# Strassen's algorithm for gate tiles of three float32 feed-forwards on one Trainium2 core

## The chip, the cores and the metric
One core of one Trainium2 chip runs the whole program. The metric is the device time of one execution in microseconds, as the median of the runs; less is better.

## What is computed
A sequence of 512 tokens of width 1024, in float32, goes through two blocks: a first one (pooling mixer, spatial gating, a feed-forward with a short convolution, a gated projection) and a second one of two layers, each with a SwiGLU feed-forward, attention, and another SwiGLU feed-forward. The change is about the last three of these four SwiGLU feed-forwards, called s1, s2 and s3 in the kernel (s0 is the first):

```python
D_FF = 2816
def swiglu(h, wg, wu, wd):
    return (jax.nn.silu(h @ wg) * (h @ wu)) @ wd
...
x = x + 0.5 * swiglu(rmsnorm_2(x, ffn_norm2[i]), ffn2_wg[i], ffn2_wu[i], ffn2_wd[i])
```

## The kernel before, in words
**Data.** The activations stay in SBUF transposed: `X` is 8 chunks of 128 channels by 512 tokens. A float32 product is made of three fp32r products: every operand is split into a high part (a ScalarE copy that rounds, `Hh`, `Ph`, `Wh`) and a low part (the rest, by a VectorE subtraction, `Hl`, `Pl`, `Wl`), and `mm3` (L1186 to L1188) issues high x low, low x high and high x high. `H` holds the normed input of a feed-forward, `P` the hidden activations.

**Weights.** All weights are a list of tiles of 1 MB at most (`weight_tiles`). SyncE loads tile n into `RAW[n % 2]` as soon as the low part of tile n - 2 is made (L2632). The step `split` makes its high part on ScalarE in two halves (L1565) and its low part on VectorE (L1928; on GpSimd, L2495, in the attention stages) into region n % 3 of `Wh` and `Wl`, once tile n - 3 is used up.

**A feed-forward** (`ffn`, L338) goes through the 22 chunks of 128 hidden channels in `THIRDS` of 8, 8 and 6. A third is first four (or three) pairs: pair (h, j) takes a gate tile `a` and a value tile `b`, each 1024 x 256, and makes two banks of each, a bank being 128 hidden channels by 512 tokens, from 8 k-blocks x 3 = 24 matmuls (`dense`). Then come four down-projection tiles `d`, whose two banks each are added to `X` (`add_x`, L2160).
For every pair: VectorE multiplies each bank by the norm factor R (`scale`, L1995; R lies in `M[:, 6]` and is made at the start of the feed-forward, ScalarE's part of it is L1611); ScalarE applies silu from the bank into a `TMP` tile (`silu`, L1682); VectorE multiplies by the value bank (`glu`, L2139); ScalarE makes the high half in `Ph` (`pair`, L1628), VectorE the low half in `Pl` (L1916).

**What sets the order.** `order` writes one list of steps by hand; each engine's program goes through the same list and issues its own part of every step. So each engine works strictly in the order of the list, and a step that waits keeps everything behind it on its engine waiting. Semaphore waits are worked out from named events. PSUM banks (8) and `TMP` tiles (3) are taken from rings; a taker waits until the last holder is done. Small other work is put in between: `norm_step` after each bank (in the last third of s3 it is `x_turn`, four PE transposes at L1362 and a ScalarE copy at L1706), and `extra` before a pair (in s1 the steps `trig` and `tables`, L2191 to L2227, before pair (0, 1)).
The sums of squares for the next norm are added on GpSimd (`stats`, L2502; a second sum L2509). Other lines in the rows: L1821 and L2450 are a ScalarE copy and a VectorE subtraction of half a bank in the second attention, L2169 and L2174 VectorE operations of the stage before s0.

## Time and profile before
| | us |
|---|---|
| median of 3 runs | 2660.2 |
| lowest, highest run | 2658.64, 2660.27 |
| profiled execution, first to last instruction (span) | 2659.0 |
| PE busy in the span | 2630.2 |
| DVE, ACT, POOL busy | 1437.9, 987.7, 320.2 |

The profiler's own execution is given by its span; the page lists no other time of it, and the runs' times stand beside it. PE is TensorE (PEld its weight loads), DVE VectorE, ACT ScalarE, POOL GpSimd, SP SyncE. Matmuls are pipelined: a row's duration is longer than the step from one start to the next, and it is the step (the pitch) that adds up to the span. The page gives times by engine, by line and by group of instructions; the timelines give single instructions with their start; "idle before <- releaser" names what an engine waited for.

### The profile page before, as it was taken

The numbers are of one execution on the slowest core, as the hardware profiler recorded it, in microseconds if no ns is written. First come the engines' busy times: TensorE is split into PE (matmuls) and PEld (weight loads), VectorE is DVE, ScalarE is ACT, GpSimd is POOL, SyncE is SP. The second block draws the span as 40 slices with busy tenths as digits, with TensorE's granted clock in tenths as the row PEclk, the third lists the DMA queues.
The fourth block names the chain that finished last, engine by engine and source line by source line (L and its number), as shares of the span: only waits on it lengthen the run. The fifth ranks groups of instructions, "written<-read, shape, count | busy, mean of one in ns | idle before, by whom it ended". The sixth has DMA issues, their size and how long they took to land.

```text
span 2659.0 us, 30833 instructions
## 1 busy us (share of the span) xinstructions
PE 2630.2 (99%) x12546; PEld 2197.8 (83%) x12560; DVE 1437.9 (54%) x2266; ACT 987.7 (37%) x1626; POOL 320.2 (12%) x388
## 2 busy tenths in 40 slices
PE   9999999999999999999999999999999989999999
PEld 8888888888887788889988888888888788888887
DVE  7637547574757444356774343453434676543433
ACT  4334334242454222246642222422223586432221
POOL 0000010000021000015530000100000586200000
PEclk9999999999999999999999999999999999999999
DMA  5332225423232444453323222232222101232222
GB/s 161 121 101 80 95 79 190 154 85 106 80 101 90 107 103 107 98 109 104 104 96 110 95 95 88 88 111 95 95 95 83 61 19 42 88 109 95 95 91 68
DMA packets 276389, 258.91 MB, mean 97 GB/s; under 512 B 40324, under 2 KB 266647, under 8 KB 276247
## 3 DMA queue, kind: packets, MB, share of 16 engines
q1 hardware_dynamic: 276231, 256.93, 31.6%
q8 instruction: 99, 1.62, 0.2%
q14 instruction: 43, 0.35, 0.0%
q10 hardware_dynamic: 16, 0.00, 0.0%
HBM read 242.23 MB, written 14.68 MB: 97 GB/s over the span
## 4 chain that ended last, share of the span: by engine, by line
PE 90%; DVE 3%; ACT 3%; issue 2%; POOL 2%; DMA 0%; SPq 0%; POOLq 0%; DVEq 0%; ACTq 0%
PE bank L1186 29%; PE bank L1188 29%; PE bank L1187 29%; PE bank L1353 1%; DVE Wl L1928 1%; ACT Wh L1565 0%; PE bank L1417 0%; POOL Wl L2495 0%; ACT Z L1851 0%; POOL TMP L2502 0%; DVE Pl L2450 0%; PE bank L1285 0%; PE bank L1513 0%; ACT Hh L1841 0%; PE bank L1197 0%
## 5 line engine op out<-in xcount | busy, mean ns | idle before, releaser
L1186 PE MATMUL bank<-Hh,Wl 128*128 128x512 f32 x2136 | 838.9, 393 | 0.8 <-DVE Hl L1947 0.8
L1188 PE MATMUL bank<-Hh,Wh 128*128 128x512 f32 x2136 | 832.3, 390 | 0.0
L1187 PE MATMUL bank<-Hl,Wh 128*128 128x512 f32 x2136 | 831.8, 389 | 0.0
L1928 DVE TENSOR_TENSOR Wl<-RAW,Wh 128x1024 fp32r<-128x1024 f32 (+2 forms) x420 | 493.7, 1219 | 171.2 <-ACT Wh L1565 170.4
L1565 ACT ACTIVATE Wh<-RAW 128x1024 fp32r<-128x1024 f32 (+2 forms) x454 | 441.2, 1022 | 382.8 <-PE bank L1188 358.4
L1186 PEld LDWEIGHTS bank<-Hh,Wl 128*128 128x128 f32 x2136 | 401.4, 188 | 86.8 <-issue 1.7
L1187 PEld LDWEIGHTS bank<-Hl,Wh 128*128 128x128 f32 x2136 | 401.5, 188 | 84.0 <-issue 1.7
L1188 PEld LDWEIGHTS bank<-Hh,Wh 128*128 128x128 f32 x2136 | 401.2, 188 | 83.9
L1186 PE MATMUL bank<-Ph,Wl 128*128 128x512 f32 x1152 | 451.9, 392 | 0.8 <-DVE Wl L1928 0.5
L1188 PE MATMUL bank<-Ph,Wh 128*128 128x512 f32 x1152 | 448.6, 389 | 0.0
L1187 PE MATMUL bank<-Pl,Wh 128*128 128x512 f32 x1152 | 448.2, 389 | 0.0
L1995 DVE TENSOR_TENSOR bank<-bank,M 128x512 f32<-128x512 f32 x220 | 150.6, 697 | 387.9 <-PE bank L1188 379.2
L2502 POOL TENSOR_TENSOR TMP<-TMP 128x512 f32<-128x512 f32 x56 | 78.2, 1396 | 1822.1 <-ACT TMP L1592 1820.9
L1186 PEld LDWEIGHTS bank<-Ph,Wl 128*128 128x128 f32 x1152 | 216.3, 188 | 47.4 <-DVE Wl L1928 0.9
L1188 PEld LDWEIGHTS bank<-Ph,Wh 128*128 128x128 f32 x1152 | 216.2, 188 | 45.4
L2160 DVE SCALAR_TENSOR_TENSOR X<-bank,X 128x512 f32<-128x512 f32 x168 | 114.9, 688 | 256.3 <-PE bank L1188 255.7
L1187 PEld LDWEIGHTS bank<-Pl,Wh 128*128 128x128 f32 x1152 | 216.3, 188 | 44.7 <-issue 0.2
L1628 ACT ACTIVATE Ph<-TMP 128x512 fp32r<-128x512 f32 x110 | 69.5, 632 | 463.6 <-DVE TMP L2139 410.4
L1682 ACT ACTIVATE TMP<-bank 128x512 f32<-128x512 f32 x88 | 52.2, 599 | 224.4 <-DVE bank L1995 224.3
L1916 DVE TENSOR_TENSOR Pl<-TMP,Ph 128x512 fp32r<-128x512 f32 x126 | 87.2, 692 | 77.6 <-ACT Ph L1628 76.8
L1583 ACT ACTIVATE Hh<-X,P 128x512 fp32r<-128x512 f32 x64 | 45.7, 722 | 102.5 <-DVE X L2160 101.1
L2495 POOL TENSOR_TENSOR Wl<-RAW,Wh 128x1024 fp32r<-128x1024 f32 (+1 forms) x34 | 74.6, 2216 | 27.4 <-ACT Wh L1565 23.2
(336 smaller groups left out, 2427.4 us busy)
## 6 DMA issues: line engine op xcount, KB each, us to landing
RAW<-in_ffn_wg SPq DMA_DIRECT2D x44, 1024.0 KB, 5.2
RAW<-in_ffn_wu SPq DMA_DIRECT2D x44, 1024.0 KB, 5.2
RAW<-in_ffn_wd SPq DMA_DIRECT2D x32, 1024.0 KB, 4.8
RAW<-in_w_up SPq DMA_DIRECT2D x22, 1024.0 KB, 5.1
RAW<-in_w_in SPq DMA_DIRECT2D x20, 1024.0 KB, 5.1
RAW<-in_ffn_wd SPq DMA_DIRECT2D x16, 768.0 KB, 4.3
bias_scratch<-M SPq DMA_DIRECT2D x16, 512.0 KB, 8.0
RAW<-in_w_down SPq DMA_DIRECT2D x8, 1024.0 KB, 4.8
```

The lines of the kernel that those rows point to most:

```text
L1186: mm(o, ll, rh, start=start, stop=False)
L1187: mm(o, lh, rl, start=False, stop=False)
L1188: return mm(o, lh, rh, start=False, stop=stop)
L1565: run(Wh[:, n % 3, x:y], RAW[:, n % 2, x:y], ACT.Copy).then_inc(*w_hi.up(("w_hi", n, i)))
L1628: run(Ph[:, q, :], tmp(name) if src == "tmp" else bank(name), ACT.Copy).then_inc(*pair_hi.up(("p_hi", q, ver)))
L1682: run(vacant(t), bank(b), ACT.Silu).then_inc(*act_out.up(("silu", t), free=b))
L1916: tt(Pl[:, q, :], src, f(Ph[:, q, :]), ALU.subtract).then_inc(*pair_lo.up(("p", q, ver), free=free))
L1928: tt(Wl[:, n % 3, x:y], RAW[:, n % 2, x:y], f(Wh[:, n % 3, x:y]), ALU.subtract).then_inc(*w_lo.up(*([("w_lo", n)] if i else [])))
L1995: tt(bank(b), bank(b), RVIEW[norm_R[nv]], ALU.mult).then_inc(*dve_out.up(("scaled", b)))
L2160: stt(X[:, c, :], bank(b), factor, X[:, c, :], ALU.mult, ALU.add).then_inc(*x_new.up(("x", ver, c), free=b))
L2495: tt(Wl[:, n % 3, x:y], RAW[:, n % 2, x:y], f(Wh[:, n % 3, x:y]), ALU.subtract).then_inc(*w_lo_pool.up(*([("w_lo", n)] if i else [])))
L2502: tt(SQ, SQ, tmp(("t_sq", nv, c)), ALU.add).then_inc(*pool_out.up(("sq", nv, c), free=("t_sq", nv, c)))
```

## The change
In s1, s2 and s3 the gate tiles from pair (0, 2) on are computed by one level of Strassen's algorithm (Winograd's form). The tile's k-blocks, its 256 hidden channels and the 512 tokens are each halved, and instead of eight block products there are seven (`PRODUCTS`), each of 4 k-blocks x 3 matmuls of 256 columns. They need four sums of weight blocks (`w_sum`, `w_sum4`, on GpSimd, from `RAW`), four sums of activation blocks for each r (`hc_sum`, made once at the start of a feed-forward, on GpSimd for even r and on VectorE for odd r, from scaled float32 copies `hc_raw` that ScalarE makes, and split into high and low by `hc`), and sums of the results. The results are built up in three half-used banks: fx takes products 1, 6, 7 and 4 one on top of the other, with ScalarE copying it away in between (`cp`), fz takes product 2, fy 5 and 3; VectorE adds the pieces (`c11`, `c12`, `c22`) into `TMP`, GpSimd multiplies by R there (`rm`; `c21` has it with it), and silu runs in place (`silu_f`). PE's products 6, 7 and 4 wait for the copies 1, 2 and 3, and product 3 for c22.

The value tiles and the down projection keep their matmuls. The order of the steps is new (`ffn_seven` for `ffn`). The weight regions are handed out differently (`places`): in a feed-forward value tiles always have the region `other`, gate tiles the region `mid`, and the fourth piece of a Strassen tile goes into `WS`. `Ph` and `Pl` 8 to 15 hold the activation sums, so a third always uses `P` 0 to 7. `feed` issues the sums and splits of gate tile n + 2 during pair n. The diff, cut:

```diff
+SEVEN = ("s1", "s2", "s3")
+FIRST_SEVEN = (0, 2)
+PRODUCTS = {1: (0, 0, 0, "fx"), 2: (0, 1, 1, "fz"), 3: (3, 0, 2, "fy"), 4: (2, 1, 6, "fx"), 5: (1, 0, 3, "fy"),
+            6: (1, 1, 5, "fx"), 7: (2, 0, 4, "fx")}
+PIECE_DONE = {0: (1, 2), 1: (5, 6), 2: (7, 4), 3: (3,)}
```

The regions (`places`) and the new helpers of `order`:

```diff
+        tag, x = name[:-1], name[-1]
+        if tag not in SEVEN:
+            regions = regions[1:] + regions[:1]
+            pieces = [(2048 * regions[2], 2048)]
+        else:
+            if x == "a" and key == (0, 0):
+                mid, other, ends = regions
+            if is_seven(tiles[n]):
+                pieces = [(2048 * ends + 1024 * side, 1024), (2048 * mid, 1024), (2048 * mid + 1024, 1024)]
+                side = 1 - side
+            else:
+                region = mid if x == "a" else other if x == "b" else (ends, mid, other, ends)[key[1]]
+                pieces = [(2048 * region, 2048)]
+            if x == "d" and key[1] == 3:
+                if key[0] < 2:
+                    other, ends = ends, other
+                else:
+                    regions = [mid, other, ends]
...
+
+    def feed(n, *pieces):
+        for piece in pieces if n < NW and is_seven(tiles[n]) else ():
+            if piece == "sums":
+                do("w_sum", n)
+                continue
+            if piece == 3:
+                do("w_sum4", n)
+            do("w_fill", n, piece)
+            if piece == 3:
+                assert now["split"] == n
+                now["split"] += 1
+                load()
+
+    def plain(n):
+        if n < NW and not is_seven(tiles[n]) and now["split"] == n:
+            split()
+            load()
 
     def norm_step():
```

The new order of a feed-forward (`...` stands for lines left out):

```diff
+    def ffn_seven(tag, nver=None, after=None, after_base=0):
+        do("mark", ("up", tag))
+        gname, gbase = GAINS[tag]
+        keys = hkeys()
+        combos = []
+        for r in range(4):
+            combos.append(lambda r=r: do("hc_raw", tag, r, xv[2 * r:2 * r + 2], gname, gbase))
+            combos.append(lambda r=r: do("hc_sum", tag, r))
+        for z, r in ((4, 0), (7, 1), (10, 2), (11, 3)):
+            combos.insert(z, lambda r=r: do("hc", tag, r))
+
...
+        def prod(n, i):
+            if i in (1, 2, 5):
+                banks.take((PRODUCTS[i][3], n))
+            do("prod", n, i, tag, keys)
+
+        def pair_seven(h, j, last_pair):
+            n = next_tile(tag + "a", (h, j), 0)
+            t = [("t_a", tag, h, j, c) for c in range(2)]
+            feed(n + 2, "sums")
+            prod(n, 1)
+            prod(n, 2)
+            for c in range(2):
+                tmps.take(t[c])
+            do("cp", n, 1, t)
+            plain(n + 1)
+            do("c11", n, t)
+            norm_step()
+            prod(n, 6)
+            do("cp", n, 2, t)
+            prod(n, 5)
+            prod(n, 7)
+            do("cp", n, 3, t)
+            do("c22", n, t)
+            norm_step()
+            nb = next_tile(tag + "b", (h, j), 0)
+            bb = [(tag + "b", h, j, c) for c in range(2)]
+            if last_pair:
+                plain(n + 2)
+            else:
+                feed(n + 2, 0, 1)
+            dense([bb[0]], nb, 8, "H")
+            scale([bb[0]])
+            prod(n, 4)
+            do("c21", n, t, now["norm"])
+            prod(n, 3)
+            do("c12", n, t)
+            for m in range(2):
+                do("rm", n, m, t, now["norm"])
+            dense([bb[1]], nb, 8, "H", kw=1)
+            do("used", nb)
+            if last_pair:
+                plain(n + 3)
+            else:
+                feed(n + 2, 2, 3)
+            for m in range(2):
+                do("silu_f", n, m, t)
+            for m in range(2):
+                if m:
+                    scale([bb[1]])
+                do("glu", t[m], bb[m])
+                pair_p(2 * j + m, "tmp", t[m], ("glu", t[m]))
+
+        def pair_eight(h, j):
+            begins = (h, j) == (0, 0)
+            ba, bb = ([(tag + x, h, j, c) for c in range(2)] for x in "ab")
+            na = next_tile(tag + "a", (h, j), 1)
+            dense(ba, na, 8, "H", scaled=not begins, wide=begins)
+            do("used", na)
+            if begins:
+                norm_step()
+                combine(2)
+                nb = next_tile(tag + "b", (h, j), 1)
+                feed(na + 2, "sums")
+                dense(bb[0:1], nb, 8, "H")
+                combine(2)
+                dense(bb[1:2], nb, 8, "H", kw=1)
+                do("used", nb)
+                scale(ba)
+                feed(na + 2, 0)
+            for c in range(2):
+                t = tmps.take(("t_a", tag, h, j, c))
+                do("silu", ba[c], t)
+            if begins:
+                combine(2)
+                feed(na + 2, 1, 2, 3)
+                scale(bb)
+            else:
+                nb = next_tile(tag + "b", (h, j), 1)
+                feed(na + 2, "sums", 0)
+                combine(3)
+                dense(bb[0:1], nb, 8, "H")
+                scale(bb[0:1])
+                feed(na + 2, 1)
+                combine(2)
+                dense(bb[1:2], nb, 8, "H", kw=1)
+                do("used", nb)
+                feed(na + 2, 2, 3)
+                scale(bb[1:2])
+            for c in range(2):
+                t = ("t_a", tag, h, j, c)
+                do("glu", t, bb[c])
+                pair_p(2 * j + c, "tmp", t, ("glu", t))
+            if begins:
+                combine(2)
+
+        for h, (c0, n) in enumerate(THIRDS):
+            last = (tag, h) == ("s3", 2)
+            if last:
+                todo[:] = [lambda i=i: x_turn(i // 4, i % 4) for i in range(8)]
+            for j in range(n // 2):
+                if (h, j) != (0, 0):
+                    extra(4)
+                if (h, j) >= FIRST_SEVEN:
+                    assert not combos
+                    pair_seven(h, j, j == n // 2 - 1)
+                else:
+                    pair_eight(h, j)
+            if h == 2:
+                h_new(tag + "_after")
+                do("mark", ("mfree", tag))
+            for i in range(4):
+                extra(4)
+                nd = next_tile(tag + "d", (h, i))
+                if last:
+                    out_rows(i, nd, n // 2, 0)
+                    continue
+                bd = [(tag + "d", h, i, c) for c in range(2)]
+                dense(bd, nd, n, "P", base=0, wide=i == 0)
+                do("used", nd)
+                if h < 2 and i == 2:
+                    feed(nd + 2, "sums", 1, 2)
+                if h < 2 and i == 3:
```

What the engines do for the new steps, PE first, then ACT, DVE and POOL:

```diff
+            elif kind == "prod":
+                n, i, tag, keys = s
+                piece, part, x, region = PRODUCTS[i]
+                name = (region, n)
+                begins = i in (1, 2, 5)
+                pe.wait_ge(*at(("w_lo", n, piece)))
+                o = (vacant(name) if begins else bank(name))[:, 0:256]
+                if i == 6 or i == 7 or i == 4:
+                    pe.wait_ge(*at(("cp", n, {6: 1, 7: 2, 4: 3}[i])))
+                elif i == 3:
+                    pe.wait_ge(*at(("c22", n)))
+                wh, wl = (w[:, 512 * part:512 * part + 512] for w in piece_of(n, piece))
+                for r in range(4):
+                    pe.wait_ge(*at(("hc_lo", tag, r) if x > 2 else keys[2 * r + min(x, 1)]))
+                    xh, xl = moving(r, x)
+                    rr = slice(128 * r, 128 * r + 128)
+                    mm(o, wl[:, rr], xh, start=begins and r == 0, stop=False, skip_group_check=True)
+                    mm(o, wh[:, rr], xl, start=False, stop=False, skip_group_check=True)
+                    ins = mm(o, wh[:, rr], xh, start=False, stop=r == 3, skip_group_check=True)
+                ins.then_inc(*bank_full.up(("prod", n, i)))
...
+            elif kind == "w_fill":
+                n, piece = s
+                act.wait_ge(*at(("sum", n, piece) if piece else ("raw", n)))
+                for event in released(n, piece):
+                    act.wait_ge(*at(event))
+                if piece == 3:
+                    all_gone(("up", tiles[n][0][:-1]))
+                run(shaped(piece_of(n, piece)[0], piece), piece_source(n, piece), ACT.Copy).then_inc(
+                    *w_hi.up(("w_hi", n, piece)))
+            elif kind == "hc_raw":
+                tag, r, xver, gname, base = s
+                for c in (2 * r, 2 * r + 1):
+                    act.wait_ge(*at(("x", xver[c % 2], c)))
+                all_gone(("up", tag))
+                if r > 1:
+                    act.wait_ge(*at(("hc_lo", tag, r - 2)))
...
+            elif kind == "hc":
+                tag, r = s
+                act.wait_ge(*at(("hc_raw", tag, 2 * r + 1)))
+                act.wait_ge(*at(("hc_sum", tag, r)))
+                all_gone(("up", tag))
+                run(Ph[:, 8 + 2 * r:10 + 2 * r, :], hc_sums(r), ACT.Copy).then_inc(*pair_hi.up(("hc_hi", tag, r)))
+            elif kind == "cp":
+                n, k, t = s
+                m = int(k == 3)
+                act.wait_ge(*at(("prod", n, {1: 1, 2: 6, 3: 7}[k])))
+                v = tmp(t[m]) if k == 2 else vacant(t[m])
+                z = 0 if k == 1 else 256
+                run(v[:, z:z + 256], bank(("fx", n))[:, 0:256], ACT.Copy).then_inc(*act_out.up(("cp", n, k)))
+            elif kind == "silu_f":
+                n, m, t = s
+                act.wait_ge(*at(("rm", n, m)))
+                act.wait_ge(*at(("c21", n)))
+                run(tmp(t[m]), tmp(t[m]), ACT.Silu).then_inc(*act_out.up(("silu", t[m])))
...
+            elif kind == "w_fill":
+                n, piece = s
+                wh, wl = piece_of(n, piece)
+                dve.wait_ge(*at(("w_hi", n, piece)))
+                tt(shaped(wl, piece), piece_source(n, piece), f(shaped(wh, piece)), ALU.subtract).then_inc(
+                    *w_lo.up(("w_lo", n, piece), *([("w_lo", n)] if piece == 3 else [])))
...
+            elif kind == "hc":
+                tag, r = s
+                q = slice(8 + 2 * r, 10 + 2 * r)
+                dve.wait_ge(*at(("hc_hi", tag, r)))
+                tt(Pl[:, q, :], hc_sums(r), f(Ph[:, q, :]), ALU.subtract).then_inc(*pair_lo.up(("hc_lo", tag, r)))
...
+            elif kind == "c22":
+                n, t = s
+                v = tmp(t[1])[:, 256:512]
+                dve.wait_ge(*at(("cp", n, 3)))
+                dve.wait_ge(*at(("prod", n, 5)))
+                tt(v, bank(("fy", n))[:, 0:256], v, ALU.add).then_inc(*dve_out.up(("c22", n)))
+            elif kind == "c12":
+                n, t = s
+                v = tmp(t[0])[:, 256:512]
+                dve.wait_ge(*at(("cp", n, 2)))
+                dve.wait_ge(*at(("prod", n, 3)))
+                tt(v, bank(("fy", n))[:, 0:256], v, ALU.add).then_inc(*dve_out.up(("c12", n), free=("fy", n)))
...
+            elif kind == "w_sum":
+                n, = s
+                v = raw_blocks(n)
+                a11, a21, a22 = v[:, :, 0, 0, :], v[:, :, 0, 1, :], v[:, :, 1, 1, :]
+                n1, n2 = (NS[:, z:z + 512].rearrange("p (r m) -> p r m", r=4) for z in (0, 512))
+                pool.wait_ge(*at(("raw", n)))
+                for event in gone(("up", tiles[n][0][:-1])):
+                    pool.wait_ge(*event)
+                if seven_before(n) is not None:
+                    pool.wait_ge(*at(("w_lo", seven_before(n), 1)))
+                tt(n1, a21, a22, ALU.add).then_inc(*w_sum.up(("sum", n, 0)))
+                pool.wait_ge(*at(("sum", n, 0)))
+                tt(n2, n1, a11, ALU.subtract).then_inc(*w_sum.up(("sum", n, 1)))
+                tt(a21, a11, a21, ALU.subtract).then_inc(*w_sum.up(("sum", n, 2)))
+            elif kind == "w_sum4":
+                n, = s
+                a12 = raw_blocks(n)[:, :, 1, 0, :]
+                n2 = NS[:, 512:1024].rearrange("p (r m) -> p r m", r=4)
+                pool.wait_ge(*at(("sum", n, 1)))
+                pool.wait_ge(*at(("w_lo", n, 0)))
+                tt(a12, a12, n2, ALU.subtract).then_inc(*w_sum.up(("sum", n, 3)))
...
+            elif kind == "rm":
+                n, m, t, nv = s
+                z = 256 * m
+                v = tmp(t[m])[:, z:512]
+                pool.wait_ge(*at(("c22", n) if m else ("c12", n)))
+                if m == 0:
+                    pool.wait_ge(*at(("c11", n)))
+                pool.wait_ge(*at(("R", nv)))
+                tt(v, v, RVIEW[norm_R[nv]][:, z:512], ALU.mult).then_inc(*pool_out.up(("rm", n, m)))
```

The sums over the activation blocks:

```diff
+    def combos(eng, tt, out_, tag, r):
+
+        b11_12, b21_22 = ((tag, 2 * r), (tag, 2 * r + 1))
+        eng.wait_ge(*at(("hc_raw",) + b11_12))
+        tt(hc_block(r, 4), hc_block(r, 1), hc_block(r, 0), ALU.subtract).then_inc(*out_.up(("hc_t1", tag, r)))
+        eng.wait_ge(*at(("hc_raw",) + b21_22))
+        tt(hc_block(r, 5), hc_block(r, 3), hc_block(r, 1), ALU.subtract).then_inc(*out_.up())
+        eng.wait_ge(*at(("hc_t1", tag, r)))
+        tt(hc_block(r, 6), hc_block(r, 3), hc_block(r, 4), ALU.subtract).then_inc(*out_.up(("hc_t2", tag, r)))
+        eng.wait_ge(*at(("hc_t2", tag, r)))
+        tt(hc_block(r, 7), hc_block(r, 2), hc_block(r, 6), ALU.subtract).then_inc(*out_.up(("hc_sum", tag, r)))
```

## Rows read from the trace of the kernel before
**Rows 1.** the page: busy time of the engines, and the chain that ended last
```profile
PE 2630.2 (99%) x12546; PEld 2197.8 (83%) x12560; DVE 1437.9 (54%) x2266; ACT 987.7 (37%) x1626; POOL 320.2 (12%) x388
...
PE 90%; DVE 3%; ACT 3%; issue 2%; POOL 2%; DMA 0%; SPq 0%; POOLq 0%; DVEq 0%; ACTq 0%
```
**Rows 2.** table by stretches, s1: busy us (x instructions), granted clock, DMA share, GB/s
```profile
1364.90:1725.80 360.90, 360.90 (x1598) 298.57 (x1596) 165.93 (x227) 103.24 (x132) 9.41 (x7) 1.00 0.30 98
```
**Rows 3.** timeline of PE in s1: start us, us, engine, line, operation
```profile
1499.65 0.39 PE L1188 MATMUL bank<-Hh,Wh 128*128 128x512 f32 x1
...
1511.89 0.39 PE L1188 MATMUL bank<-Hh,Wh 128*128 128x512 f32 x1
```
**Rows 4.** timeline of PE in the first attention, half-width matmuls
```profile
1227.21 0.28 PE L1186 MATMUL bank<-Wh,Hl 128*128 128x256 f32 x1
...
1229.97 0.28 PE L1188 MATMUL bank<-Wh,Hh 128*128 128x256 f32 x1
```
**Rows 5.** groups by line and form in s1, busy us, mean ns, idle before
```profile
L1565 ACT ACTIVATE Wh<-RAW 128x1024 fp32r<-128x1024 f32 x60 | 60.0, 1049 | 69.7 <-PE bank L1188 63.4 <-DMA RAW<-in_ffn_wu 6.3
...
L1928 DVE TENSOR_TENSOR Wl<-RAW,Wh 128x1024 fp32r<-128x1024 f32 x60 | 71.3, 1232 | 22.0 <-ACT Wh L1565 22.0
```
**Rows 6.** groups by line and form, whole span, operations of 256 columns
```profile
L1821 ACT ACTIVATE TMP<-bank 128x256 f32<-128x256 f32 x16 | 6.2, 385 | 1.1 <-DVE pkf L2392 1.0
...
L2450 DVE TENSOR_TENSOR Pl<-bank,Ph 128x256 fp32r<-128x256 f32 x16 | 6.6, 415 | 0.7 <-ACT Ph L1860 0.7
```
**Rows 7.** groups by line and form, POOL: in s1, and over the span
```profile
L2502 POOL TENSOR_TENSOR TMP<-TMP 128x512 f32<-128x512 f32 x7 | 9.4, 1344 | 348.9 <-ACT TMP L1592 348.9
...
L2495 POOL TENSOR_TENSOR Wl<-RAW,Wh 128x1024 fp32r<-128x1024 f32 x26 | 62.2, 2417 | 22.4 <-ACT Wh L1565 18.2 <-DVE M L2276 2.8 <-DVE sm L2317 1.4
```
**Rows 8.** timeline of DVE and POOL where both read two SBUF tensors
```profile
787.01 0.80 DVE L2169 TENSOR_TENSOR TMP<-TMP,M 128x512 f32<-128x512 f32 x1 [1.79 <-ACT TMP L1701]
...
787.22 1.75 POOL L2509 TENSOR_TENSOR Z<-Z,TMP 128x512 f32<-128x512 f32 x1
...
787.84 1.67 DVE L2174 TENSOR_TENSOR X<-X,TMP 128x512 f32<-128x512 f32 x1
```
**Rows 9.** timeline of DVE and ACT, the end of a pair in s1
```profile
1508.24 0.70 DVE L1995 TENSOR_TENSOR bank<-bank,M 128x512 f32<-128x512 f32 x1 [4.74 <-PE bank L1188]
...
1508.85 0.68 DVE L2139 TENSOR_TENSOR TMP<-TMP,bank 128x512 f32<-128x512 f32 x1
...
1509.56 0.63 ACT L1628 ACTIVATE Ph<-TMP 128x512 fp32r<-128x512 f32 x1 [8.97 <-DVE TMP L2139]
...
1510.22 0.69 DVE L1916 TENSOR_TENSOR Pl<-TMP,Ph 128x512 fp32r<-128x512 f32 x1 [0.70 <-ACT Ph L1628]
```
**Rows 10.** timelines of DVE and ACT, first two pairs of s1, s2, s3
```profile
1382.27 0.16 DVE L2191 CAST sm<-smi 128x4 f32<-128x4 int32 x1
...
1387.01 2.36 DVE L1928 TENSOR_TENSOR Wl<-RAW,Wh 128x1024 fp32r<-128x1024 f32 x2
...
1733.09 0.60 ACT L1611 ACTIVATE M<-bank 128x512 f32<-128x512 f32 x1 [5.18 <-PE bank L1301]
...
1738.57 0.70 DVE L1995 TENSOR_TENSOR bank<-bank,M 128x512 f32<-128x512 f32 x1 [2.34 <-PE bank L1188]
...
2314.97 0.60 ACT L1611 ACTIVATE M<-bank 128x512 f32<-128x512 f32 x1 [9.61 <-PE bank L1301]
...
2325.90 0.70 DVE L1995 TENSOR_TENSOR bank<-bank,M 128x512 f32<-128x512 f32 x1 [0.61 <-PE bank L1188]
```
**Rows 11.** timeline, one x_turn in the last third of s3: PE, then ACT
```profile
2577.40 0.60 PE L1362 MATMUL bank<-ident,X 128*128 128x128 f32 x4
...
2578.04 0.60 ACT L1706 ACTIVATE M<-bank 128x512 f32<-128x512 f32 x1 [5.33 <-PE bank L1362]
```
**Rows 12.** table by stretches, after the ple stage and in the second attention
```profile
823.00:827.00 4.00, 4.00 (x17) 3.36 (x17) 3.69 (x13) 0.14 (x1) 0.00 (x0) 0.66 0.75 236
2115.00:2135.00 20.00, 14.65 (x115) 13.79 (x114) 15.40 (x45) 17.80 (x54) 17.23 (x28) 1.00 0.16 54
```

135 lines of the change are left out of this document (115 added, 20 removed).

## The prediction
> **What bounds the kernel now.** The page first: TensorE (PE) is busy 99% of the span of 2659.0 us, and the chain that ended last runs through it for 90% [rows 1]. Then the table by stretches: over s1, the first of the three feed-forwards that the change touches, PE is busy for all of 360.90 us at granted clock 1.00, VectorE (DVE) for 165.93, ScalarE (ACT) for 103.24 and GpSimd (POOL) for 9.41 [rows 2]. The waits list no wait of PE from 1364 to 2082 us nor from 2302 us on. So in these stages the time is the number of matmuls times their pitch, and everything else has slack. A busy PE isn't the whole story of the change, though: it makes PE wait for ACT in the middle of a pair, so the order of ACT's and DVE's queues has to be read as well.
>
> **What is saved.** Pitch is start to start. With 512 columns: 54 steps from 1499.65 to 1511.89 us, 0.2267 us each [rows 3]. With 256 columns: 23 steps from 1227.21 to 1229.97, 0.120 us each [rows 4]; the half-size matmul costs 53%, not 50%. A gate tile was 48 matmuls of 512 columns, 10.88 us; it becomes 7 products of 12 matmuls of 256 columns, 84 x 0.120 = 10.08 us. Saved: 0.80 us. Nine of the 11 pairs of each feed-forward are treated so, three times: 27 x 0.80 = 21.6 us. That is all the change can bring, 0.8%.
>
> The Trainium skill, "TensorE: Matmul & The Clock Gate", section "Back-to-back issue gap", gives N/2.4 + 2.5 ns for a warm matmul. By it the tile would save 1.19 us and the change 32 us, called an estimate; both traced pitches are above that rule, so the traced ones are taken.
>
> **What a pair does to the queues.** Set t = 0 at the first product of a pair. PE: products 1 and 2 (1.44 us each) to 2.88; 6, 5, 7 to 7.20; first value bank to 12.64; products 4, 3 to 15.52; second value bank to 20.96. Product 6 adds to the bank that ACT must first have copied (cp 1). That copy stands in ACT's queue behind the whole tail of the pair before, so I follow that tail from the end of product 3 (pitch end X) to cp 1 of the next pair. PE leaves 8.32 us for it (second value bank 5.44, products 1 and 2 2.88). Durations stand in [rows 5 to 7, 9]; a follower on the same engine starts 0.09 before the former's end, one on another engine 0.03 to 0.05 after it:
> - c12 on DVE starts at X+0.19 (last matmul's tail and hop), as scale does after its bank; 0.42.
> - w_fill 2's low half is next on DVE (its inputs are ready) and starts at X+0.52, before POOL's rm 0, which waits for c12's end. It takes 1.22 and reads two SBUF tensors, as rm 0 does. [Rows 8] shows what that means: DVE's TMP,M operation at 787.01 stretches POOL's of 787.22 to 1.75 instead of 1.34 us [rows 7], so that this one really begins 0.18 before DVE's recorded end; and the next DVE one, at 787.84, waits for POOL (1.67 instead of 0.69). One instruction at a time has the path. So rm 0 really starts at X + 0.52 + 1.22 - 0.18 = X+1.56.
> - rm 0 1.34, rm 1 (256 columns, 0.81 by the slope between 512 and 1024), w_sum4 1.34, less two overlaps, and the hop to ACT: X+5.02.
> - ACT w_fill 3 high 0.63, DVE its low half 0.69 (ACT's silu runs beside it): X+6.37. Then glu 0, pair high 0, pair low 0, scale and glu 1, pair high 1: 0.59+0.66+0.72+0.52+0.68+0.66; together X+10.20.
> - cp 1 0.39 less 0.09, hop 0.05: X+10.55.
>
> PE therefore waits 10.55 - 8.32 = 2.2 us at product 6. Nothing behind it makes this good, for the same chain starts again at product 3: a pair takes 20.96 + 2.2 = 23.2 us, where it took 96 x 0.2267 = 21.76. Inside the pair I find no further wait over 0.2 us: cp 2 has product 5 to hide under, cp 3 and c22 the first value bank, and the value tile's split ends just before its bank is due.
>
> The skill's "SBUF — State Buffer", section "Who interferes with whom", says that a DVE instruction with two SBUF inputs contends with a GpSimd one that reads SBUF, the later one waiting for the whole of the other. That rule speaks against this change, and [rows 8] bear it out. Without the effect rm 0 would start at X+0.69, 0.87 us sooner, and the sum below would be 14 us less.
>
> **How often.** Such a tail precedes a Strassen pair 6 times in a feed-forward: once in third 0, three times in third 1, twice in third 2. After down projections ACT's queue is empty and cp 1 is in time. The last pair of a third hides its tail under the first six of eight (or four of six) k-blocks of the down projection, 8.2 or 5.4 us. Of the 18, two are worse: in s3's last third an x_turn follows each dense call, so ACT waits for the four transposes behind the second value bank (0.60) and copies (0.60) [rows 11] before it may start w_fill 2, 3 and silu. Worked through in the same way these two cost 4.5 and 4.9 us. Sum: 16 x 2.2 + 9.4 = 44.6 us.
>
> **The first two pairs.** They now carry the activation sums: 8 ACT copies like a pair's high half (0.63 [rows 9]), four of 1.05 [rows 5], 8 combinations of 0.42 [rows 6] and four low halves of 1.23 [rows 5] on DVE, 8 combinations of 0.8 [rows 7] on POOL. And the value tile of pair (0,1) now shares a region with that of (0,0), so its split comes only after all this. In s2, the last value bank of pair (0,0) ends at 1738.57 - 0.19; the tile is due 10.88 us later, at 1749.26. From the copy of R, which stood at 1733.09 [rows 10], the queue has two copies, four combinations, two scales, hc 0, raw 2, two glu/pair rounds, hc 1 and the two Wl halves: done at 1749.2. Just in time, but POOL's three weight sums (4.0 us) now fall into the same 5 us, and with one reader at a time two of them delay it: 2.6 us late. In s1 the trig steps stand before the split (1382.27 to 1387.01 [rows 10]): 4.7 late. In s3 R comes later (2314.97) and the tile is due at 2325.71 [rows 10]: 3.4, with the sums 6.0. Together 13.3 us.
> After that DVE has 10.9 us of work under 10.9 us of matmuls, then scale, glu 0, pair, glu 1, pair, cp 1, 4.2 + 1.3 us against the 2.88 of products 1 and 2: 2.6 us at each of three feed-forwards, 7.8.
>
> **The sum.** 44.6 + 13.3 + 7.8 - 21.6 = +44.1 us: the profiled span 2659.0 becomes 2703. The median, 2660.2, stands 1.2 us above the profiled span, so I forecast 2704 us.
>
> Bounds. POOL's operations are untraced for these operands: with the one-tensor-and-column form they could be shorter, and if the collision with w_fill 2 and with the sums fell away the forecast drops by 14 + 5 us, to 2685. If also the beginnings hid themselves, 2666. Upwards: POOL operations of 1.64, between the 1.34 and the 1.75 of [rows 7, 8], add 0.3 x 3 x 16 = 14 us. A halved clock is the other one: after PE's weak stretch at 822 us the granted clock is 0.66 in the mean of 4 us, so at its lower level, 1.2 GHz, for most of them, with some 1.4 us lost; against it, 14.65 busy in 20 us with waits up to 2.3 left it at 1.00 [rows 12]. None is in the sum; one for each of some seven long waits adds 10 us. An unseen gain in the beginnings has no room, PE not having waited there.
>
> **Rivals.**
> A. The tail hides: POOL and ACT are early enough, or the order leaves cp 1 free, and only 21.6 us of matmuls are left out: 2660.2 - 21.6 = 2639, faster. For it: DVE is 46% and ACT 29% busy in s1 [rows 2], so there is ample capacity. Against it: the wait is one of order, not of capacity. The point from which it decides: all waits together must be under 21.6 us, that is under 0.8 us a pair; my chain has 2.2 and would need to be 1.4 us shorter everywhere and the beginnings nearly free.
> B. Near break-even: no collision on the read path and no waits at the beginnings, chain 1.2 us late: 16 x 1.2 + 9.4 for the x_turns + 3 x 1.0 - 21.6 = +10, 2670; with a little less, no measurable change.
> C. Clock drops at every wait of 2.2 us too: 16 x 1.4 + 10 more, about 2736. For it: row 823 to 827; against it: the attention stretch.
> D. The 256-column matmuls are held by weight loads, one for each, at a pitch above 0.120. At 0.130 the saving is gone (84 x 0.130 = 10.92) and the time about 2727. [Rows 4] speak against it: these matmuls too change their weights every time.
>
> **How the numbers follow.** Forecast with its bounds (2685 to 2730) 0.64; rival A 0.12; B 0.13, of which 0.05 within 0.2%; C 0.05; D 0.06. 0.2% (5.3 us) is about what a measurement of this kernel can tell from no change. Faster 0.12, same 0.05, slower 0.83. The range for 8 in 10 leaves out A and C and reaches into B: 2665 to 2734.
>
> **What would show it.** Right: PE waits for ACT (the copy of bank fx) some 16 times at 2 to 2.5 us and longer twice in s3's last third; ahead of each such copy ACT's pair copy, ahead of that DVE's glu; POOL's rm 0 listed at 2.2 us rather than 1.3 where it starts behind w_fill 2; PE waits for DVE Wl once in each feed-forward's second pair; matmuls of 256 columns at 0.12; each feed-forward about 15 us longer. Wrong: no PE wait at product 6, feed-forwards of 353 us instead of 360; waits that sit at product 7 or 4 or at the value bank would mean that another link is late; a granted clock under 0.98 in the stages would be C.

## The result: 2734.0 us, and the profile after

The changed kernel takes 2734.0 us in the median of five runs (2733.0 to 2736.7), against 2660.2 for the kernel before: a ratio of 1.028, 95% interval 1.0267 to 1.0292. The direction was as forecast; the forecast was +44 us, the outcome +74. The profiled execution is the longest of the five (2736.7 us) and has a span of 2735.5 us, 76.5 more than before's 2659.0.

The page of the changed kernel, busy times and the chain that ended last, beside [rows 1]:

```profile
PE 2645.6 (97%) x13532; PEld 2254.5 (82%) x13532; DVE 1572.2 (57%) x2410; ACT 1084.5 (40%) x1797; POOL 598.2 (22%) x574
...
PE 70%; issue 9%; DVE 7%; POOL 7%; ACT 4%; DMA 3%; POOLq 0%; SPq 0%; ACTq 0%; DVEq 0%
```

TensorE is busy 15 us longer, though 21.6 us of its work were to be saved. That is the first sign that something besides waiting has been added. The second is the granted clock in the table by stretches of s1 and s3 (columns as in [rows 2]: busy of PE, PEld, DVE, ACT, POOL, then the clock), where [rows 2] had 1.00:

```profile
1364.90:1736.00 371.10, 349.22 (x1860) 303.34 (x1859) 206.07 (x270) 131.56 (x183) 98.14 (x66) 0.98 0.30 94
...
2350.00:2735.50 385.50, 356.92 (x1879) 310.27 (x1877) 191.73 (x224) 120.76 (x169) 87.81 (x58) 0.96 0.26 85
```

The waits of PE (engine line <- releaser: us in all, times, longest). L1564 is the first matmul of a product, L1464 that of a dense bank:

```profile
PE bank L1564 <- ACT TMP L1897: 43.9, 18, 5.0
PE bank L1464 <- DVE Wl L2267: 17.3, 7, 7.1
...
PE bank L1564 <- issue: 4.4, 3, 1.5
```

L1897 is the copy cp 1. It is waited for 18 times: 16 times for 2.15 us, and in s3's last third for 4.53 and 4.97 us. The other nine waits in s1 to s3 belong to the first pairs: 7.10, 1.47 and 0.42 us in s1, 2.36, 1.48 and 0.84 in s2, 5.84, 1.48 and 0.34 in s3 (the smallest of each at the first value bank of pair (0,2)). All 27 make 16 x 2.15 + 9.50 + 21.33 = 65.2 us.

Here is one tail, link by link, merged from the timelines of the four engines in s1:

```profile
1517.82 0.42 DVE L2301 TENSOR_TENSOR TMP<-bank,TMP 128x256 f32<-128x256 f32 x1 [1.01 <-PE bank L1566]
1518.16 1.22 DVE L2273 TENSOR_TENSOR Wl<-RAW,Wh 128x1024 fp32r<-128x1024 f32 x1
1518.32 2.91 POOL L2908 TENSOR_TENSOR TMP<-TMP,M 128x512 f32<-128x512 f32 x2 [12.36 <-DVE TMP L2301]
1521.19 1.29 POOL L2895 TENSOR_TENSOR RAW<-RAW,M 128x512 f32<-128x512 f32 x1
1522.51 0.63 ACT L1872 ACTIVATE WS<-RAW 128x512 fp32r<-128x512 f32 x1 [5.01 <-POOL RAW L2895]
1523.18 0.69 DVE L2273 TENSOR_TENSOR WS<-RAW,WS 128x512 fp32r<-128x512 f32 x1 [3.80 <-ACT WS L1872]
1523.79 0.68 DVE L2518 TENSOR_TENSOR TMP<-TMP,bank 128x512 f32<-128x512 f32 x1
1524.50 0.63 ACT L1965 ACTIVATE Ph<-TMP 128x512 fp32r<-128x512 f32 x1 [0.31 <-DVE TMP L2518]
...
1527.22 0.63 ACT L1965 ACTIVATE Ph<-TMP 128x512 fp32r<-128x512 f32 x1 [2.09 <-DVE TMP L2518]
1527.76 0.37 ACT L1897 ACTIVATE TMP<-bank 128x256 f32<-128x256 f32 x1
...
1528.27 0.36 PE L1564 MATMUL bank<-Ph,Wl 128*128 128x256 f32 x1 [2.15 <-ACT TMP L1897]
```

c12, w_fill 2's low half, rm 0 and rm 1 (one row, x2), w_sum4, w_fill 3, glu 0, pair high 0, pair high 1, cp 1, product 6: the order of the prediction, nothing in another place. ACT stands idle for 5.01 us and again for 2.09 us in it, and DVE for 3.80: waits of order, while all three engines have room.

What the prediction had not in its sum is seen behind such a wait. PE's timeline behind the wait that ends at 1438.87, and behind the one of 1528.27:

```profile
1438.87 0.35 PE L1564 MATMUL bank<-Ph,Wl 128*128 128x256 f32 x1 [2.15 <-ACT TMP L1897]
...
1440.01 0.41 PE L1564 MATMUL bank<-Ph,Wl 128*128 128x256 f32 x1
1440.23 0.41 PE L1565 MATMUL bank<-Pl,Wh 128*128 128x256 f32 x1
...
1528.94 0.28 PE L1566 MATMUL bank<-Ph,Wh 128*128 128x256 f32 x1
1529.06 0.28 PE L1564 MATMUL bank<-Ph,Wl 128*128 128x256 f32 x1
```

The step from start to start is 0.12 us in the second case and 0.213 in the first: the lower clock level, 1.2 GHz, for 15 matmuls (1439.37 to 1442.57), and 1.57 us lost with the slower first ones. In the table by stretches the same two places read 0.66 and 1.00 (the column behind POOL's):

```profile
1438.00:1443.00 5.00, 4.13 (x22) 4.16 (x23) 3.39 (x4) 3.01 (x5) 0.00 (x0) 0.66 0.16 49
1528.00:1533.00 5.00, 4.73 (x38) 4.72 (x39) 4.37 (x4) 2.51 (x5) 3.66 (x2) 1.00 0.08 26
```

The two waits are equally long. Of the 16 of 2.15 us, 8 are followed by the lower clock; so are all five longer ones (2.36 to 7.10 us), with 1.7 to 3 us lost behind each. And each wait costs 0.15 us more than the row lists as idle: the last start before 1528.27 is 2.43 us earlier, 2.31 more than the pitch.

**The balance.** The matmuls should take 21.6 us less, the waits add 65.2 and the restarts 27 x 0.15 = 4.1. Of the 76.5 us that leaves 76.5 + 21.6 - 65.2 - 4.1 = 28.8 us. The slow matmuls of the timelines give 8 x 1.57 = 12.6, and 2.2, 1.7, 3.0, 3 and 2.75 behind the five long waits, together about 25. The rest, some 3.5 us, lies in part outside s1 to s3: the copy of R in s1, which stands at 1372.20 us in the profile before, stands at 1373.81 here, behind a stretch of lower clock that before's profile hasn't (0.76 over 1243 to 1250 us, where before has 1.00) in a stage that the change doesn't touch. In the other kernels' profiles that copy stands between 1370.8 and 1372.5, so I take this for a difference between executions.

```profile
1243.00:1250.00 7.00, 5.43 (x33) 5.44 (x34) 4.95 (x17) 4.58 (x16) 4.00 (x6) 0.76 0.93 255
```

What is left are matmuls slower by 0.1 us right behind a wait and what I can't assign. From the copy of R in s1 to that in s2 it is 23.8 us more than before, from there to that in s3 (with the second attention) 18.0, and from there to the end 33.1; the forecast had about 15 for each feed-forward.

### The profile page after: what moved, and what is told of

The parts are those of the page before. It is cut to its first block, busy times and chain, and to the rows that moved or that the text cites. A ratio compares the mean times of both kernels' runs of the same rounds, so it can differ in the third digit from the quotient of the medians.

```text
span 2735.5 us, 33395 instructions
## 1 busy us (share of the span) xinstructions
PE 2645.6 (97%) x13532; PEld 2254.5 (82%) x13532; DVE 1572.2 (57%) x2410; ACT 1084.5 (40%) x1797; POOL 598.2 (22%) x574
## 4 chain that ended last, share of the span: by engine, by line
PE 70%; issue 9%; DVE 7%; POOL 7%; ACT 4%; DMA 3%; POOLq 0%; SPq 0%; ACTq 0%; DVEq 0%
PE bank L1464 21%; PE bank L1466 21%; PE bank L1465 21%; DMA RAW<-in_ffn_wg 3%; PE bank L1564 1%; PE bank L1565 1%; PE bank L1566 1%; POOL M L2887 1%; POOL TMP L2908 1%; POOL M L2885 1%; POOL RAW L2895 1%; DVE Wl L2267 1%; POOL RAW L2888 1%; PE bank L1651 1%; DVE bank L2374 1%
## 5 line engine op out<-in xcount | busy, mean ns | idle before, releaser
L1464 PE MATMUL bank<-Hh,Wl 128*128 128x512 f32 x1704 | 674.7, 396 | 17.7 <-DVE Wl L2267 16.9
L1465 PE MATMUL bank<-Hl,Wh 128*128 128x512 f32 x1704 | 667.0, 391 | 0.0
L1466 PE MATMUL bank<-Hh,Wh 128*128 128x512 f32 x1704 | 666.5, 391 | 0.0
L2267 DVE TENSOR_TENSOR Wl<-RAW,Wh 128x1024 fp32r<-128x1024 f32 (+1 forms) x366 | 473.1, 1335 | 138.2 <-ACT Wh L1864 137.6
L1464 PE MATMUL bank<-Ph,Wl 128*128 128x512 f32 x1152 | 451.9, 392 | 0.8 <-DVE Wl L2267 0.4
L1464 PEld LDWEIGHTS bank<-Hh,Wl 128*128 128x128 f32 x1704 | 322.2, 189 | 87.8 <-DVE Wl L2267 19.2
L1466 PEld LDWEIGHTS bank<-Hh,Wh 128*128 128x128 f32 x1704 | 321.7, 189 | 68.5
L1465 PEld LDWEIGHTS bank<-Hl,Wh 128*128 128x128 f32 x1704 | 322.3, 189 | 65.7 <-issue 1.7
L1464 PEld LDWEIGHTS bank<-Ph,Wl 128*128 128x128 f32 x1152 | 216.3, 188 | 47.1 <-DVE Wl L2267 0.9
L1564 PE MATMUL bank<-Ph,Wl 128*128 128x256 f32 x432 | 131.9, 305 | 48.3 <-ACT TMP L1897 43.9
L2908 POOL TENSOR_TENSOR TMP<-TMP,M 128x512 f32<-128x512 f32 (+1 forms) x54 | 83.8, 1572 | 355.1 <-DVE TMP L2301 355.1
L1564 PEld LDWEIGHTS bank<-Ph,Wl 128*128 128x128 f32 x432 | 90.9, 210 | 53.0 <-issue 52.0
```

The lines of the kernel that those rows point to most:

```text
L1464: mm(o, ll, rh, start=start, stop=False)
L1465: mm(o, lh, rl, start=False, stop=False)
L1466: return mm(o, lh, rh, start=False, stop=stop)
L1564: mm(o, wl[:, rr], xh, start=begins and r == 0, stop=False, skip_group_check=True)
L2267: tt(wflat(Wl, o + x, o + y), RAW[:, n % 2, x:y], f(wflat(Wh, o + x, o + y)), ALU.subtract).then_inc(*w_lo.up(*([("w_lo", n)] if i else [])))
L2908: tt(v, v, RVIEW[norm_R[nv]][:, z:512], ALU.mult).then_inc(*pool_out.up(("rm", n, m)))
```

## The experiments

Eleven kernels, each an edit of the changed kernel (2734.0 us); the times are medians, the ratios are to the kernel before, measured alongside (its medians were 2658.8 to 2660.2 us, so a difference of 1 or 2 us between two of these kernels tells nothing).

| run | us | ratio, 95% interval | what is left |
|---|---|---|---|
| pair copy late | 2671.5 | 1.0045 (1.0028 to 1.0061) | 25.9 us of waits |
| w_sum4 early | 2692.1 | 1.012 (1.0105 to 1.0135) | the 2.15 us waits gone |
| 18 extra matmuls | 2716.3 | 1.0216 (1.02 to 1.0231) | same chain, PE kept busy |
| one reader | 2704.6 | 1.0167 (1.0152 to 1.0183) | waits of 1.22 us |
| split early | 2740.8 | 1.0306 (1.0291 to 1.032) | waits moved and grown |
| x_turns before | 2726.6 | 1.0249 (1.0235 to 1.0263) | 4.5 and 5.0 become 1.7 and 2.15 |
| all the orders | 2662.9 | 1.0013 (1.0004 to 1.0022) | 3 waits of 5.7 to 6.1 us |
| all, from fourth pair | 2643.4 | 0.994 (0.9926 to 0.9953) | one wait of 0.55 us |
| 4 extra matmuls | 2722.3 | 1.0234 (1.0213 to 1.0254) | 16 waits of 1.58 us |
| 2 extra matmuls | 2733.7 | 1.0277 (1.0256 to 1.0297) | 16 waits of 1.82 us |
| from fourth alone | 2714.8 | 1.0202 (1.0185 to 1.0219) | see below |

A slip in the first four expectations: they count 13 waits of 2.15 us; the profile has 16, and 8 clock losses, not nine. With 16 and 8 (and the long waits as they have them) their theories give 2679, 2701, 2719 and 2708 us, where they say 2685, 2703, 2718 and 2709.

### Is it one chain, and does it run through the second pair copy?

```diff
             do("c11", n, t)
+            while late:
+                late.pop()()
...
-                pair_p(2 * j + m, "tmp", t[m], ("glu", t[m]))
+                if m and not last_pair:
+                    late.append(lambda: pair_p(2 * j + 1, "tmp", t[1], ("glu", t[1])))
+                else:
+                    pair_p(2 * j + m, "tmp", t[m], ("glu", t[m]))
```

> Base: the changed kernel, 2734 us. Edit: between two Strassen pairs of a third, the second pair copy (ACT high half, DVE low half) is queued behind cp 1 and c11 of the next pair. Theory (one chain): cp 1 then follows pair high 0, which ends before product 1 does, so the 13 waits of 2.15 us at product 6 vanish (13 x 2.31 with the restart = 30 us; the other three of the 18 tails precede the first pairs of s1 to s3's Strassen part and were never 2.15) and the two of 4.53 and 4.97 us in s3's last third shrink by 2.6 each (5 us); the clock lost behind the 2.15 us waits (nine times 1.57 = 14 us) goes with them: about 2685 us, stage clock back to 1.00 in s1's and s2's windows but for their beginnings. Rival 1 (the clock is lost for a cause of its own, such as the small matmuls): waits go, the clock loss stays, 2699 us. Rival 2 (another link, the POOL sums or DVE, is as late): waits at product 6 stay above 1.2 us, 2710 us or more.

Measured 2671.5 us, 62.5 less. ACT's timeline at the same place, in this run (L1972 is the pair copy, L1904 cp 1):

```profile
1517.76 0.63 ACT L1972 ACTIVATE Ph<-TMP 128x512 fp32r<-128x512 f32 x1 [0.31 <-DVE TMP L2525]
1518.29 0.37 ACT L1904 ACTIVATE TMP<-bank 128x256 f32<-128x256 f32 x1
```

cp 1 now follows pair high 0 at once, and all 16 waits are gone; in s3's last third 1.81 and 2.25 us are left of 4.53 and 4.97. By the span, 2669.8, 65.7 us were won: 39.3 of waits, 2.6 of restarts, and so 23.8 of clock, 3 us of it ahead of s1 (the copy of R stands at 1370.79 here). The clock loss went with the waits; rival 1 would have stood at 2692 (2734 - 42) and is out, and so is rival 2. With 16 waits and 8 losses my sum would have been 2679; the 7 us below it are the clock behind the two long waits (about 5.7 us), which I had let stand, and that behind s2's wait of 2.36 us, which this time cost none.

The other way into the same chain:

```diff
+            if not last_pair:
+                feed(n + 2, "sum4")
             do("c12", n, t)
             for m in range(2):
                 do("rm", n, m, t, now["norm"])
```

> Edit: w_sum4 is queued on POOL ahead of c12 and the rm's, in the first value bank's time. Theory: it stood in the chain with 1.3 us (wait for it, then fill 3, silu, glu), so the waits of 2.15 us become 0.85 us: 13 x 1.3 = 17 us less. If a wait as short as 0.85 us costs no clock, nine times 1.57 = 14 us go as well: 2703 us. If the clock falls behind any wait, only the 17 go: 2717 us. Rival (POOL isn't in the chain, ACT and DVE are): waits stay 2.15, 2734 us.

Measured 2692.1 us, 41.9 less, more than the 1.3 us a pair that I allowed. PE's waits in this run:

```profile
PE bank L1467 <- DVE Wl L2270: 21.3, 13, 7.1
PE bank L1567 <- ACT TMP L1900: 9.5, 2, 5.0
```

Not one of the 16 waits of 2.15 us at product 6 is left: w_fill 3's two halves (0.63 and 0.69 us in the tail above) stood behind w_sum4 and left the chain with it, so 2.6 us went, not 1.3. In 8 of the 16 places PE now waits 0.5 to 0.8 us at the next value bank, for the split of its tile: the next link. The two waits of 4.53 and 4.97 us are unchanged, since there the x_turn holds ACT. The measured size again includes the clock: 16 x 2.3 = 37 us of waits and their restarts less some 6 us for the 8 new ones with theirs, and so about 11 us of clock.

### The read path of rm 0

```diff
+                if piece == 2:
+                    tt(wl[:, 0:16], wh[:, 0:16], wh[:, 0:16], ALU.subtract).then_inc(*w_lo.up(("w_lo", n, piece)))
+                    continue
```

> Edit, and what it leaves out: of the low half of the third piece of each Strassen weight tile DVE writes 16 columns only (0.1 us instead of 1.22 us), so nothing on DVE reads two SBUF tensors while POOL's rm 0 runs. Theory (one reader of the shared path at a time): rm 0 starts at the end of c12 and takes 1.35 us where it showed 2.1, the chain is 0.85 us shorter, waits of 2.15 become 1.3 us: 13 x 0.85 = 11 us less, 2723 us, and 2709 us if waits of 1.3 us cost no clock. Rival (rm 0 has this duration by itself): rm 0 stays at 2.1 us, waits at 2.15, 2734 us.

Measured 2704.6 us, 29.4 less. DVE and POOL at the same place, in this run (L2304 is c12, L2274 the low half cut to 16 columns, L2911 rm 0 and rm 1, L2898 w_sum4):

```profile
1515.24 0.42 DVE L2304 TENSOR_TENSOR TMP<-bank,TMP 128x256 f32<-128x256 f32 x1 [1.01 <-PE bank L1566]
1515.58 0.16 DVE L2274 TENSOR_TENSOR Wl<-Wh 128x16 fp32r<-128x16 f32 x1
...
1515.74 1.99 POOL L2911 TENSOR_TENSOR TMP<-TMP,M 128x512 f32<-128x512 f32 x2 [12.44 <-DVE Wl L2274]
1517.69 1.29 POOL L2898 TENSOR_TENSOR RAW<-RAW,M 128x512 f32<-128x512 f32 x1
```

The same two POOL instructions take 1.99 us instead of 2.91 (rm 0 1.29 instead of 2.21, rm 1 0.74 in both), and w_sum4 starts 2.45 us behind c12's start instead of 3.37. The edit also makes DVE free 1.1 us sooner, but that isn't what shortened the chain: in the changed kernel DVE stands idle for 3.80 us further down in it. All 16 waits became 1.22 us, 0.93 shorter, where I had worked out 0.87. With 0.6 us at each of the two long ones that makes 16.1 us. The remaining 13.3 us are the clock: not one of the 16 waits of 1.22 us is followed by a slow matmul.

### The clock by itself

```diff
+            banks.take(("fy", n))
+            if now.get("tail"):
+                do("filler", n)
+            now["tail"] = not last_pair
             prod(n, 6)
...
+            elif kind == "filler":
+                n, = s
+                pe.wait_ge(*at(("w_lo", n, 1)))
+                o = vacant(("fy", n))[:, 0:256]
+                for _ in range(18):
+                    mm(o, piece_of(n, 1)[0][:, 512:640], Hh[:, 0, 0:256], start=True, stop=True, skip_group_check=True)
```

> Edit: 18 extra matmuls of 256 columns (18 x 0.12 = 2.16 us of TensorE, result thrown away by the next start in that bank) ahead of product 6, where a Strassen pair precedes. Nothing else is sooner: the chain to cp 1 is the same, so the time can fall only by what the clock and the restart cost. Theory (the halved clock is brought on by the idle time alone): the nine losses of 1.57 us and the restarts (13 x 0.15) go, 2734 - 14 - 2 = 2718 us. Rival (the clock falls for something other than the idle time): unchanged, 2734 us or a little more. The two waits of s3's last third shrink to 2.4 and 2.8 us without gain in time.

Measured 2716.3 us, 17.7 less, with 18 matmuls more in each of 18 pairs. Nothing is earlier in this kernel; PE only isn't idle any more. So some 15 us of the loss, beside 2.5 us of restarts, are the price of being idle and not of the idle time itself. The two waits of s3's last third shrank to 2.29 and 2.72 us, and no stretch of lower clock follows them either. This is the run that settles it: the clock loss in the tails is brought on by the waits, and neither by the small matmuls, of which there are more in this kernel, nor by anything in the products.

The last two runs of this kind ask from which length on, with 4 and 2 extra matmuls:

> As the run with 18 extra matmuls ahead of product 6, with 4 (0.48 us): the 16 waits of 2.15 us become 1.67 us, and nothing else is sooner. Waits of 1.2 and 1.5 us have cost no clock so far, waits of 2.15 us did in 8 of 16. If 1.67 us belongs to the harmless ones, the eight losses of 1.57 us go: 2734 - 12.6 = 2721 us. If the loss falls off gradually with the wait, some three to six of them stay: 2726 to 2731 us. If any idle time between 1.5 and 2.15 us costs the same: 2734 us.

> The same with 2 extra matmuls (0.24 us): waits of 1.91 us. Same three theories: 2721 us if these cost no clock, 2734 us if about half of them do as at 2.15 us, between the two if the share falls off.

Measured 2722.3 and 2733.7 us; the waits became 1.58 and 1.82 us where I had worked out 1.67 and 1.91. PE behind the wait in s1, with 4 extra matmuls, then with 2:

```profile
1523.96 0.39 PE L1574 MATMUL bank<-Ph,Wl 128*128 128x256 f32 x1 [1.58 <-ACT TMP L1907]
1524.18 0.28 PE L1575 MATMUL bank<-Pl,Wh 128*128 128x256 f32 x1
```

```profile
1527.13 0.39 PE L1574 MATMUL bank<-Ph,Wl 128*128 128x256 f32 x1 [1.82 <-ACT TMP L1907]
...
1527.69 0.41 PE L1574 MATMUL bank<-Ph,Wl 128*128 128x256 f32 x1
```

Behind 1.58 us none of 16 has a row of slow matmuls (the first or the first two are 0.1 us slow, as behind every wait), behind 1.82 us 9 of 16 have. That is as many as behind 2.15 us, so between 1.58 and 2.15 us the share doesn't fall off gradually.

### The first two pairs

```diff
                 do("used", nb)
+                plain(nb + 2)
                 scale(ba)
```

> Edit: in the first pair the split of the value tile of pair (0,1) is queued right behind the last use of the tile of pair (0,0), ahead of scale, silu, sums and combinations. Theory 1 (the order alone makes it late): the waits of 7.1, 2.4 and 5.8 us at that tile's bank go, with the clock lost behind them (6.9 us by the profile of the changed kernel): 2734 - 15.8 - 6.9 = 2711 us. Theory 2 (DVE's whole work in the first two pairs is too long, its order matters little): TensorE comes to product 6 of pair (0,2) sooner and waits there instead, 5 to 8 us in s1, 3 to 5 in s2 and s3 where it was 1.5; what is won is DVE's idle gaps, 2 to 3 us in each feed-forward: 2725 us. My prediction took theory 1 for the first waits and 2.6 us at each (0,2) besides.

Measured 2740.8 us: 6.8 us slower than the changed kernel, so theory 1 is out, and even theory 2 was too hopeful. PE's waits in this run:

```profile
PE bank L1565 <- ACT TMP L1898: 43.9, 18, 5.0
PE bank L1565 <- issue: 23.6, 3, 8.1
...
PE bank L1565 <- DVE Wl L2274: 3.9, 1, 3.9
```

The tile of (0,1) is in time, and PE now waits 7.84, 7.70 and 8.08 us at product 6 of (0,2), where 1.5 stood ("issue" here: the profile shows no release that came last; ahead of it in s1 ACT's cp 1 ends, at 1416.02). In s1 the 3.9 us are a further wait, at product 1 of (0,2), for the first piece of its weights, which now stands behind the trig steps and a scale. It is not DVE's amount of work alone: from the copy of R to product 6 of (0,2) DVE is busy for 31.7, 26.7 and 25.1 us in s1, s2 and s3 (PE for 31.3, 29.5 and 24.1) of 43.0, 37.2 and 32.1 us. It has about as much to do as PE, and 7 to 11 us of idle time besides, most of it behind copies of ACT. That whatever is put first makes something else late is how I read it; the split put first also delays scale and silu.

```diff
-FIRST_SEVEN = (0, 2)
+FIRST_SEVEN = (0, 3)
```

> One number of the change alone: Strassen's products begin with pair (0,3) instead of (0,2), the order of the tail as in the change. Theory (the waits at the beginning are DVE's work of the first two pairs, and a third pair takes them up): 9 waits of 21.3 us together and their restarts (1.4 us) go and the clock lost behind them (some 7 us), against 2.4 us less saved: 2734 - 29.7 + 2.4 = 2707 us; with DVE's tail now running into pair (0,3), where 2.15 us stood, waits of 1.5 to 2.2 us stay there. Rival (the late tile has another cause than that work): TensorE still waits 5 us or more within pairs (0,1) to (0,3) of s1 and s3, 2725 us or more.

Measured 2714.8 us, between the two. s2's late tile is in time with a third ordinary pair; s1 still waits 4.84 us (the trig steps still stand ahead of the split there) and s3 3.63. At product 6 of (0,3) PE waits 1.48 us where it waited 2.15, as the theory has it. So in s1 and s3 order and amount both count, and neither theory held alone.

### The x_turns

```diff
             do("c22", n, t)
             norm_step()
+            norm_step()
...
+            held_back = todo[:]
+            todo[:] = []
             dense([bb[1]], nb, 8, "H", kw=1)
+            todo[:] = held_back
```

> Edit: in s3's last third the x_turn that followed the second value bank is done with the one behind c22, so ACT has no copy of transposes between the end of product 3 and cp 1. Theory (the two long waits are the common chain plus x_turn): 4.53 and 4.97 us become 2.15 us, -5.2 us, and the clock lost behind them falls from 3 and 2.75 us to 1.5 or nothing: 2725 us. Rival (x_turn isn't in that chain): both waits unchanged, 2734 us.

Measured 2726.6 us, 7.4 less. The two waits became 1.71 and 2.15 us, as the theory has it, and the first of them lost no clock.

### Everything together

> All the edits on the order together: pair high 1 behind cp 1 (also between pairs (0,1) and (0,2)), w_sum4 early, the value tile's split early, x_turn before the value bank, and no side steps (trig, tables) in the first third's first four pairs. The run with the late pair copy stands at 2671.5 us with 26 us of TensorE waits left at these places and 3 to 8 us of clock behind them. Theory 1 of the early split: all of them go, 2660.2 - 21.6 = 2639 us, faster than the kernel before by 0.8%. Theory 2: waits of 2 to 4 us are left at product 6 of (0,2) in each feed-forward, with some clock loss: about 2650 us.

> The same edits, and Strassen's products begin with the fourth pair of each feed-forward (0,3) instead of the third: 24 gate tiles instead of 27, so the activation sums have one pair more in which to be made. If DVE's work in the first pairs is what still makes TensorE wait, this beats the other: 2660.2 - 24 x 0.80 = 2641 us and waits of 0 to 1 us in each feed-forward, 2643 us. If the first pairs are no bound, it is 2.4 us slower than the version with 27 tiles.

With 27 Strassen tiles and all the orders mended 2662.9 us, 0.1% slower than the kernel before. One wait is left in each feed-forward, at product 6 of (0,2), 5.71, 5.72 and 6.09 us, each with 1.4 to 2.6 us of clock: larger than my 2 to 4 us, so that this kernel is 13 us above the slower of the two forecasts. With 24 tiles, beginning at (0,3), 2643.4 us, 0.6% faster than the kernel before and 3.3% faster than the changed one; forecast 2643. The table by stretches of this last kernel in s1 and s2, with PE busy throughout and the clock at 1.00 again:

```profile
1364.90:1715.00 350.10, 349.55 (x1855) 302.31 (x1855) 209.75 (x271) 133.01 (x184) 94.53 (x62) 1.00 0.32 101
1736.00:2080.00 344.00, 344.00 (x1841) 297.40 (x1839) 206.38 (x254) 130.54 (x183) 103.22 (x71) 1.00 0.31 97
```

DVE is busy for 210 of 350 us in it, more than in the changed kernel's share, and that costs nothing: it was never DVE's load that made PE wait outside the first two pairs.

## Why the prediction was off in size, point by point

- **What is saved**, 0.80 us a tile: right. The 24 tiles of the kernel from the fourth pair on should save 19.2 us; its span is 16.9 us under before's, with one PE wait of 0.55 us left in s1 to s3, and with a granted clock of 0.83 over 2100 to 2130 us, in the second attention, where before's profile has 1.00 throughout. Rival D is out: the small matmuls go at 0.12 us (1524.76 to 1525.84 in ten rows of the changed kernel, 0.12 each). The Trainium skill, "TensorE: Matmul & The Clock Gate", section "Back-to-back issue gap", gives N/2.4 + 2.5 ns for an isolated warm matmul, an estimated 0.109 us here, and says that this is too little at small N once each matmul loads its weights; the trace agrees, with 0.120 here and in [rows 4].
- **The tail**: 2.2 us forecast, 2.15 found, with every link in its place; the "one copy late" and "w_sum4 early" runs cut it at two of them. The share of the collision in it, on the shared read path, was 0.93 us (0.87 in the sum). The Trainium skill, "SBUF — State Buffer", section "Who interferes with whom", says that a DVE instruction with two SBUF inputs contends with a GpSimd one that reads SBUF; the 2.21 and 1.29 us of rm 0 agree with it. The working of this term has a slip: as they are listed, the items from rm 0 to the hop to ACT make X+4.92 and not X+5.02, so the wait should have come out at 2.1 us.
- **How often**: 16 and the two in s3's last third at 4.5 and 4.9: found 16, 4.53 and 4.97.
- **The first two pairs**: 13.3 + 7.8 = 21.1 us, found 21.3, but by luck of signs: s1's late tile cost 7.1 and not 4.7, s2's 2.4 and s3's 5.8 as forecast (2.6 and 6.0), and (0,1) to (0,2) 1.5 each and not 2.6. PE's being late at the first gives DVE time for the second, which I summed as if they were independent. The "split early" run shows how closely the two are tied.
- **The step that failed**: "A halved clock is the other one [...] None is in the sum." It put the clock behind PE's waits at nothing in the sum and at 10 us in the upper bound. I had two rows in [rows 12] that said opposite things, 0.66 behind a weak stretch and 1.00 over 20 us with waits up to 2.3 (the longest is in fact 2.55 us, at 2125.93), and took the one for the sum and the other for the bound, with seven losses of 1.4 us at most. The runs show that a loss (1.57 us, or 1.7 to 3 behind a long wait) follows about every second wait of 1.8 to 2.2 us and every one of 3.6 us or more: 13 losses, about 25 us, with 4 us of restarts that weren't priced either. 44 + 25 + 4 = 73, of the 76.5 us by which the profiled span is longer. One stretch of 1.00 could not exclude this: a wait of 2.15 us passes without a loss in half of the cases, and the same stretch of the attention reads 0.91 in the changed kernel's profile, where its longest wait is 2.30 us:

```profile
2158.00:2178.00 20.00, 16.33 (x116) 15.12 (x115) 15.28 (x43) 17.37 (x51) 16.96 (x28) 0.91 0.16 54
```

- **Rival C**, "clock drops at every wait", gave 2736 and stands nearest, by luck of its sizes: 16 losses at 1.4 and 10 us more, where it was 8 at 1.57 and five larger ones. Its sign, a granted clock under 0.98 in the stages, came in s3 (0.96); s1 stands at its edge (0.98).
- **Rivals A and B** needed PE's waits under 21.6 us and at about 31.6 us in all (16 x 1.2 + 9.4 + 3.0), where 65.2 were found. Less than 21.6 is reached only by the two kernels with all the orders mended (17.5 and 0.55 us).
- **The lower bound** has a slip too: from 2685, without the late tiles (13.3, of which 5 are already off) and the 7.8 behind them, it is 2669 us and not 2666. Nothing hangs on it.

## What to carry to other kernels

An idle TensorE can cost more than its idle time. In these kernels each wait cost its length plus 0.15 us; waits up to 1.6 us cost no clock, those of 1.8 to 2.2 us a loss of 1.6 us in about every second case, and those of 3.6 us and more 1.4 to 3 us each time. A change that saves matmuls and pays with side work should be checked first for what stands in another engine's queue ahead of the one short instruction that TensorE needs; here moving one copy behind it was worth 62 us, three times the arithmetic saved. And where side work is needed before its first use, starting the new scheme one step later can be worth more than the step saves: three tiles fewer cost 2.4 us and removed three waits of nearly 6 us.
